# Norm seams grown by VectorE in wider parts, and a GpSimd-only weight split beside the HGRN heads

## What is computed

```
x = x + rms_norm(mixer(rms_norm(x)))      # layer 0: HGRN2 heads | RWKV-7 heads; layer 1: retention | RG-LRU
x = x + rms_norm(swiglu(rms_norm(x)))     # every layer
rms_norm(x, w) = x * rsqrt(mean(x*x) + 1e-6) * w
```

## Time and profile before

| | |
|---|---|
| median of 3 runs | 3651.04 us (3640.59 to 3651.29) |
| the profiled execution | 3655.99 us, span 3654.0 us |
| TensorE busy | 3398.2 us, 93% of the span |
| VectorE, ScalarE, GpSimd busy | 1931.3, 1203.9, 1520.7 us |
| mean granted TensorE clock | 0.948 |

### The profile page before, as it was taken

How to read it: one execution, slowest core, us unless ns; L and a number is a source line. 1 busy time by engine, 2 the same in 40 slices (tenths; PEclk the granted TensorE clock), 3 DMA queues, 4 the chain that set the end, 5 groups by cost and what they waited for, 6 DMA issues and landing times.

```text
span 3654.0 us, 63634 instructions
## 1 busy us (share of the span) xinstructions
PE 3398.2 (93%) x24702; PEld 3263.8 (89%) x24702; DVE 1931.3 (53%) x2531; ACT 1203.9 (33%) x1492; POOL 1520.7 (42%) x888
## 2 busy tenths in 40 slices
PE   7899996858889999999999899999979999999997
PEld 7899985847879999999999799986979999999997
DVE  3544556484776442244456886724784442244456
ACT  3443443232333332233322335321233332233322
POOL 3434552000454444444443445711444445444443
PEclk9999997979899999999999999975999999999999
DMA  4333341000434444444444353532434444444443
GB/s 165 121 131 122 127 135 66 3 25 15 145 109 143 149 149 152 140 149 148 149 156 142 105 208 121 175 130 121 144 100 153 149 155 146 138 150 149 156 151 108
DMA packets 118673, 475.01 MB, mean 130 GB/s; under 512 B 13424, under 2 KB 15088, under 8 KB 115568
## 3 DMA queue, kind: packets, MB, share of 16 engines
q1 hardware_dynamic: 108864, 421.58, 34.4%
q10 hardware_dynamic: 9648, 51.17, 3.6%
HBM read 450.66 MB, written 22.03 MB: 129 GB/s over the span
## 4 chain that ended last, share of the span: by engine, by line
PE 86%; DVE 9%; ACT 3%; issue 2%; POOL 0%; ACTq 0%; DVEq 0%; POOLq 0%
PE ps L330 47%; PE ps L334 24%; DVE w_lo L306 1%; PE ps L1957 1%; PE ps L1977 1%; DVE x_lo L599 1%; PE ps L357 1%; ACT w_hi L295 1%; PE ps L362 1%; PE ps L1066 1%; PE ps L1546 1%; PE ps L1088 1%; PE ps L1495 1%; PE ps L1510 0%; PE ps L1548 0%
## 5 line engine op out<-in xcount | busy, mean ns | idle before, releaser
L306 POOL TENSOR_TENSOR w_lo<-raw,w_hi 128x512 fp32r<-128x512 f32 (+2 forms) x756 | 1389.9, 1840 | 1863.0 <-ACT w_hi L295 1857.0
L330 PE MATMUL ps<-x_hi,w_hi 128*128 128x320 f32 x4832 | 1444.6, 313 | 14.3 <-ACT w_hi L295 7.1
L330 PE MATMUL ps<-x_lo,w_hi 128*128 128x320 f32 x4832 | 1435.0, 311 | 0.0
L295 ACT ACTIVATE w_hi<-raw 128x1024 fp32r<-128x1024 f32 (+1 forms) x756 | 840.4, 1112 | 1643.0 <-PE ps L334 1545.6
L306 DVE TENSOR_TENSOR w_lo<-raw,w_hi 128x512 fp32r<-128x512 f32 (+2 forms) x692 | 630.8, 914 | 701.1 <-ACT w_hi L295 690.5
L330 PEld LDWEIGHTS ps<-x_hi,w_hi 128*128 128x128 f32 x4832 | 914.6, 189 | 23.4 <-ACT w_hi L295 12.7
L330 PEld LDWEIGHTS ps<-x_lo,w_hi 128*128 128x128 f32 x4832 | 914.3, 189 | 0.8
L334 PE MATMUL ps<-x_hi,w_lo 128*128 128x320 f32 x4832 | 811.0, 310 | 25.0 <-DVE w_lo L306 23.3
L334 PEld LDWEIGHTS ps<-x_hi,w_lo 128*128 128x128 f32 x4832 | 734.8, 188 | 31.1 <-POOL w_lo L306 19.3
L330 PE MATMUL ps<-u_hi,w_hi 128*128 128x320 f32 x1408 | 417.7, 311 | 8.3 <-DVE u_lo L711 8.3
L330 PE MATMUL ps<-u_lo,w_hi 128*128 128x320 f32 x1408 | 417.3, 310 | 0.0
(11 more groups left out here) (393 smaller groups left out, 2882.8 us busy)
## 6 DMA issues: line engine op xcount, KB each, us to landing
raw<-in_w_ffn_in SPq DMA_DIRECT2D x352, 512.0 KB, 3.4
raw<-in_w_ffn_out SPq DMA_DIRECT2D x128, 704.0 KB, 4.0
raw<-in_w_in_even SPq DMA_DIRECT2D x116, 512.0 KB, 3.5
raw<-in_w_in_odd SPq DMA_DIRECT2D x96, 512.0 KB, 3.4
raw<-in_w_out_even SPq DMA_DIRECT2D x32, 512.0 KB, 3.4
raw<-in_w_out_odd SPq DMA_DIRECT2D x32, 512.0 KB, 3.4
hS<-in_state_hgrn ACTq DMA_DIRECT2D x4, 1024.0 KB, 5.6
out_hgrn_s<-hS ACTq DMA_DIRECT2D x4, 1024.0 KB, 4.7
```

Of the source, the lines that this page charges most:

```text
L295: nc.scalar.activation(w_hi[s % 2][:, 0:g.kt, :], raw[s % 4][:, 0:g.kt, :], ACT.Copy)\
L306: eng.tensor_tensor(w_lo[s % 2][:, k0:k1, :], raw[s % 4][:, k0:k1, :], w_hi[s % 2][:, k0:k1, :].bitcast(f32), sub).then_inc(sem(f"split_lo ...
L330: nc.tensor.matmul(out, w_hi[s % 2][:, k, :], x[:, kk, :], start=half == 0 and k == 0 and x is xh, stop=False)
```

## The change

In words:

- **Seams.** VectorE does both steps of `grow` itself, in five parts of 1, 1, 2, 2 and 2 of the old ones (`SEAM_PARTS`); GpSimd no longer takes part. ScalarE weights part 0 straight into `x_hi`; for the others it writes the weighted values to `yw` (which lies in the place of `x_lo`) one tile at a time and then rounds the whole part to `x_hi` in one copy. VectorE's `low` is then a plain subtraction over the whole part. ScalarE splits units 2 and 3 together behind part 3, and squares in four instructions of four tiles behind all parts. VectorE alone sums the squares. GpSimd splits its share of units 2 onward in the ordinary loop.
- **Paired heads.** In each half the first part is taken for one unit after the other, so that TensorE begins with the first unit's `w_hi` alone.
- **HGRN.** `lo_dve` of `in_b` becomes 0: GpSimd makes all 8 tiles of each `w_lo` (128x1024). `fill_dve` goes away, VectorE raises the counter for all 100 units at the end (`pass_over`). The head of a group waits on TensorE for ScalarE's read of the state (`pse`) in place of `hgrn_end`.

The core of the diff (the code that it removes is above):

```diff
+        yw = at("yw", XHL0 + KT * T * 4, [P, KT, T])
...
-        dense("in_b", d["w_in_even"], EVEN_TILES - FIRST_TILES, KU_MODEL, 2, FIRST_TILES)
+        dense("in_b", d["w_in_even"], EVEN_TILES - FIRST_TILES, KU_MODEL, 0, FIRST_TILES)
...
         def multiply_head(pe, g, xh, xl, fill):
+            outs = [PS[(g.tile0 + t) % 4][:, 0:T] for t in range(2)]
+
+            def products(s, t, half, k, x):
+                kk = half * g.kt + k
+                if x is xh:
+                    pe.wait_ge(sem("x_hi"), 8 * fill + kk // 2 + 1)
+                else:
+                    x_lo_wait(pe, fill, kk // 2)
+                for a in range(2):
+                    nc.tensor.matmul(outs[t], w_hi[s % 2][:, k + a, :], x[:, kk + a, :],
+                                     start=kk + a == 0 and x is xh, stop=False)
+
+            if g.tile0:
+                pe.wait_ge(sem("tile_out"), g.tile0)
             for half in range(2):
                 units = (g.unit0 + 2 * half, g.unit0 + 2 * half + 1)
...
+                for t, s in enumerate(units):
+                    pe.wait_ge(sem("split_hi"), s + 1)
                     for x in (xh, xl):
+                        products(s, t, half, 0, x)
+                for k in range(2, g.kt, 2):
+                    for x in (xh, xl):
                         for t, s in enumerate(units):
+                            products(s, t, half, k, x)
...
+        SEAM_PARTS = ((0, 1), (1, 2), (2, 4), (4, 6), (6, 8))
+        NPARTS = len(SEAM_PARTS)
+
+        def span(ap, a, b):
+            return ap[:, 2 * a:2 * b, :]
+
         def seam_act(act, n, w, g):
...
+            for q, (c0, c1) in enumerate(SEAM_PARTS):
+                act.wait_ge(sem("seam_y"), NPARTS * b + q + 1)
+                for k in range(2 * c0, 2 * c1):
+                    dst = x_hi[:, k, :] if q == 0 else yw[:, k, :]
+                    ins = act.activation(dst, X[:, k, :], ACT.Copy, scale=vec(w[0], KT * w[1] + k))
+                if q == 0:
+                    ins.then_inc(sem("x_hi"), 1)
+                    continue
+                ins.then_inc(sem("seam_yw"), 1)
+                act.wait_ge(sem("seam_yw"), (NPARTS - 1) * b + q)
+                act.activation(span(x_hi, c0, c1), span(yw, c0, c1), ACT.Copy)\
+                   .then_inc(sem("x_hi"), c1 - c0)
+                if q == 3:
+                    split_hi(act, 0, g.unit0 + 2)
+                    split_hi(act, 0, g.unit0 + 3)
+            for c in range(0, 8, 2):
+                act.activation(span(M, c, c + 2), span(X, c, c + 2), ACT.Square).then_inc(sem("norm_sq"), 1)
...
-        def seam_pool(pool, n, g):
...
         def seam_dve(dve, n, w, g):
...
+            def grow(q):
+                c0, c1 = SEAM_PARTS[q]
+                x = span(X, c0, c1)
+                L(dve.tensor_tensor(x, x, bc(stat[:, 1, :].unsqueeze(1), P, 2 * (c1 - c0), T), mult))
+                dve.tensor_tensor(x, x, span(M, c0, c1), add).then_inc(sem("seam_y"), 1)
+
+            def low(q):
+                c0, c1 = SEAM_PARTS[q]
+                dve.wait_ge(sem("x_hi"), 8 * fill + c1)
+                if q == 0:
+                    for k in range(2):
+                        ins = dve.scalar_tensor_tensor(x_lo[:, k, :], X[:, k, :], vec(w[0], KT * w[1] + k),
+                                                       x_hi[:, k, :].bitcast(f32), mult, sub)
+                else:
+                    ins = dve.tensor_tensor(span(x_lo, c0, c1), span(yw, c0, c1),
+                                            span(x_hi, c0, c1).bitcast(f32), sub)
+                ins.then_inc(sem("x_lo_dve"), c1 - c0)
+
+            grow(0)
+            grow(1)
+            for q in range(NPARTS):
+                if q == 0:
+                    dve.wait_ge(sem("seam_y"), NPARTS * b + 1)
+                low(q)
+                if q + 2 < NPARTS:
+                    grow(q + 2)
+                if q == 3:
                     split_lo(dve, "dve", 0, g.unit0 + 2)
             split_lo(dve, "dve", 0, g.unit0 + 3)
             dve.tensor_scalar(sqt[:, :], PS[7][:, 0:T], RMS_EPS, RMS_EPS * RMS_EPS * D_MODEL, mult, add)
...
+            dve.wait_ge(sem("norm_sq"), 8 + 4 * b + 2)
+            L(dve.tensor_tensor(M[:, 0:4, :], M[:, 0:4, :], M[:, 4:8, :], add))
             split_lo(dve, "dve", 0, g.unit0 + 4)
...
+            for c, k in ((3, 4), (4, 4)):
+                dve.wait_ge(sem("norm_sq"), 8 + 4 * b + c)
+                L(dve.tensor_tensor(M[:, 0:4, :], M[:, 0:4, :], M[:, 4 * c - 4:4 * c, :], add))
+            L(dve.tensor_tensor(M[:, 0:2, :], M[:, 0:2, :], M[:, 2:4, :], add))
             dve.tensor_tensor(M[:, 0, :], M[:, 0, :], M[:, 1, :], add).then_inc(sem("seam_dve"), 1)
             for s in (5, 6, 7):
                 split_lo(dve, "dve", 0, g.unit0 + s)
...
-        def fill_dve(dve):
...
                 pe.wait_ge(sem("tile_out"), 8 * (g + 1))
                 if g:
-                    pe.wait_ge(sem("hgrn_end"), g)
+                    hgrn_wait(pe, "pse", g - 1)
...
-            by_stage(fill_dve(dve), itertools.chain.from_iterable(hgrn_dve(dve, g) for g in range(HGROUPS)))
+            for g in range(HGROUPS):
+                by_stage(hgrn_dve(dve, g))
+            dve.wait_ge(sem("hgrn_end"), HGROUPS)
+            pass_over(dve, plan["in_b"])
```

More of the change, by code:

```diff
@@ L11 @@
-import itertools
 import math
@@ L544, in seam_act @@
             root_act(act, n)
[L546 to L560, removed]
@@ L563, in seam_scale_act @@
+            for c in range(0, 8, 2):
+                act.activation(span(M, c, c + 2), span(X, c, c + 2), ACT.Square).then_inc(sem("norm_sq"), 1)
         def seam_scale_act(act, n):
-            act.wait_ge(sem("seam_dve"), 3 * SEAM[n] + 3)
+            act.wait_ge(sem("seam_dve"), 2 * SEAM[n] + 2)
             act.activation(srow, srow, ACT.Sqrt, scale=1.0 / D_MODEL).then_inc(sem("norm_rms"), 1)
-        def seam_pool(pool, n, g):
[L569 to L578, removed]
-                        pool.wait_ge(sem("seam_acc_pool"), 3 * b + c - 4)
-                split_lo(pool, "pool", 0, g.unit0 + s)
@@ L587, in seam_dve @@
             dve.wait_ge(sem("norm_rms"), MS[n])
-            rms = bc(stat[:, 1, :].unsqueeze(1), P, 2, T)
-            def grow(c):
-                dve.tensor_tensor(part(X, c), part(X, c), rms, mult).then_inc(sem("seam_x"), 1)
-                if c == 0:
-                    dve.wait_ge(sem("seam_x"), 8 * b + 1)
-                    dve.tensor_tensor(part(X, 0), part(X, 0), part(M, 0), add).then_inc(sem("seam_dve"), 1)
-            def low(c):
-                dve.wait_ge(sem("x_hi"), 8 * fill + c + 1)
-                for k in (2 * c, 2 * c + 1):
-                    ins = dve.scalar_tensor_tensor(x_lo[:, k, :], X[:, k, :], vec(w[0], KT * w[1] + k),
-                                                   x_hi[:, k, :].bitcast(f32), mult, sub)
-                ins.then_inc(sem("x_lo_dve"), 1)
-            for c in range(3):
-                grow(c)
-            for c in range(8):
-                if c == 0:
-                    dve.wait_ge(sem("seam_dve"), 3 * b + 1)
-                low(c)
-                if c + 3 < 8:
-                    grow(c + 3)
-                if c == 6:
+            def grow(q):
[23 more added lines that the diff above has]
+                if q == 3:
                     split_lo(dve, "dve", 0, g.unit0 + 2)
@@ L651, in last_norm_dve @@
                 if c % 2:
-                    dve.wait_ge(sem("seam_x"), 24 + c + 1)
+                    dve.wait_ge(sem("seam_x"), c + 1)
                     dve.tensor_tensor(part(X, c), part(X, c), part(M, c), add).then_inc(sem("x_new"), 1)
@@ L818, in fill_act @@
                     act.activation(sh_out[:, n, :], ps[:, 255:T:8], ACT.Copy).then_inc(sem("tile_out"), 1)
-        def fill_dve(dve):
-            g = plan["in_b"]
-            for u in range(g.units):
-                yield fill_stage(u)
-                split_lo(dve, "dve", 0, g.unit0 + u)
         def fill_pe(pe):
@@ L1998, in channel_pool @@
         def channel_pool(pool, l, after):
-            seam_pool(pool, 4 * l + 1, plan[f"up{l}0"])
             for h in range(2):
-                pool_split(pool, plan[f"up{l}{h}"], skip=0 if h else 6)
+                pool_split(pool, plan[f"up{l}{h}"], skip=0 if h else HEAD)
                 pool_split(pool, plan[f"down{l}{h}"])
@@ L2073, in _ @@
             channel_pool(pool, 0, plan["in_c"])
-            seam_pool(pool, 3, plan["in_c"])
-            pool_split(pool, plan["in_c"], skip=6)
+            pool_split(pool, plan["in_c"], skip=HEAD)
             pool_split(pool, plan["in_d"])
```

26 lines of the change are left out of this document (3 added, 23 removed).

## The result

The changed kernel takes 3618.56 us in the median of four runs (3618.26 to 3619.56), the kernel before 3651.16 beside it (3640.59 to 3655.90). The ratio is 0.9916 with a 95% interval of 0.9897 to 0.9935: 0.8% faster. The forecast was 3624 with a range of 3604 to 3642.

What follows compares the result with a forecast made beforehand. TensorE, busy 93% of the span, was taken as the bound, with time to win only where it stands. HGRN 16.3 plus three seams 11.1 made 27.4 us less: 3628.6, or 3624 carried to the median; range 3604 to 3642.

Steps and rivals of the forecast that it cites:

- TensorE's waits beside HGRN: Beside HGRN, 18.3 us of waits for VectorE's `w_lo` go; GpSimd being late costs 2 us.
- the slower rival: Beside HGRN, VectorE holds GpSimd's longer instructions, which take over some 4 us: 17 us slower, 3668; chance 0.06.
- The head wait: At the head of an HGRN group, the new wait costs nothing and brings nothing.
- `w_hi` waits "stay": Beside HGRN, the 3.4 us that TensorE waits for `w_hi` remain.
- The sum 18.3 - 2 = 16.3: HGRN stage: `w_lo` waits gone less new GpSimd delay, 16.3 us less; bounds 20 and 5 less.
- The seam's head: In each seam, the head ends 28.7 us after VectorE's first multiplication in place of 34.75, 6.0 us earlier.
- I take 2.3 us of new wait: Behind each seam's head, TensorE waits 2.3 us for unit 5's part, which stands behind VectorE's four adds of squares.
- 3.7 us less for each seam: Each seam: head 6.0 us earlier less 2.3 of new wait; 11.1 us in all for three.
- one case in which the last 28 products run low: Seam's bad bound: a 3.6 us wait and the last 28 products at low clock, 2.5 us; 0.1 lost.
- the first rival: Seams win nothing, partly as TensorE's clock there is low whenever it has stood; HGRN gives 16.3 less, 3635; chance 0.17.
- The 1.49 us of a 128x1280 step: In the seam, VectorE's 128x1280 step was put at 1.49 us, from 0.81 for 640 and 1.22 for 1024.
- the seams give nothing: Only HGRN wins, 16.3 us less, 3635, with more VectorE work and later squares in the seams; chance 0.17.
- both give their best: HGRN 20 and seams 18 us less, with no new wait behind the adds and shrunken `w_hi` waits: 3613; chance 0.20.

Runs made afterwards that it cites:

- the rest alone: The changed kernel with its HGRN edits taken back, leaving the seams and paired heads: 3647.75 us, ratio 0.9986 to the kernel before.
- narrow parts: The changed kernel with eight seam parts of two tiles each in place of the five of SEAM_PARTS: 3611.89 us, ratio 0.9892 to the kernel before.
- both orders: The changed kernel with each seam's last part ahead of unit 2 and 3 splits, and VectorE's unit 5 and 6 splits between its later adds: 3585.49 us.

## Why the prediction was right in sum, and wrong in its terms

- **TensorE's waits beside HGRN: right.** 18.3 us for VectorE's `w_lo` gone; new waits for GpSimd 3.6 - 1.7 = 1.9 us (forecast 2). The unit at each group's head is late by 0.36 to 0.41 us (forecast 0.4). GpSimd's 128x1024 takes 2.51 us in the mean from 117 to 579 us (at most 2.8 forecast), so the slower rival's condition did not come near. The head wait was worth nothing, as said.
- **`w_hi` waits "stay": failed by what was read.** From 117 us on they did (3.4, then 3.1). The longest, 3.67 us at 106.93, lay ahead of the stretch that I read. It came from VectorE's part of the first 12 units: without it 1.4 us are left there. Bringing these units back costs 2.9 us.
- **The sum 18.3 - 2 = 16.3: the step that failed.** It took waits for the whole cost, and put TensorE's busy time at nothing without a reason. Idle time fell by 18.8 us, busy time by 9.4. The 88 later units alone cost 19.7 us when brought back, 15.9 of it idle time and 3.8 busy time; the first twelve cost 2.9. That is 22.6 of the 28.2. The stage of the kernel with the rest alone is 4.0 us shorter with no HGRN edit, and 1.6 are left, less than the 2.3 by which the stage's end differs among the kernels in which GpSimd makes all of `w_lo` and VectorE does no idle work. What the busy time goes with is shown in part: of the 20 waits for `w_lo` in the kernel before only two, of 2.08 us at 116.68 and of 2.46 us at 508.87, have a clock under 1.00 in the eight microseconds behind them. So it is no price of every wait, and most of it stays open.
- **The seam's head: nearly right.** It ends 29.2 us after the first multiplication (28.7) and is 5.5 us shorter (6.0). Wide steps take 1.48 us (1.49). The new order of the products is worth nothing, as forecast for the three other heads.
- **"I take 2.3 us of new wait": right in place, 2.74 in size.** VectorE held by GpSimd was to be seen in the earlier trace rows (its instruction ended 0.28 us behind GpSimd's, not with it); its adds take 2.5 us beside GpSimd's splits. The Trainium skill (SBUF — State Buffer, Who interferes with whom) has the two engines share a port pair that one locks at a time; these adds agree, 2.5 us against 1.48 alone.
- **"3.7 us less for each seam": the other step that failed.** The idle time fell by 3.6. The busy time rose by 2.5, and 1.1 was left: 49 products ran at the lower clock where 38 had. The clock had been put into a bound, as one case in which the last 28 products run low, and not into the sum. Two places show it: the products behind the 2.74 us wait (2.47 us for eight, 1.34 usual), where moving one split wins 1.3 us of busy time, and half 0, in which narrow parts win 3.6 us without any idle time less. Nor is the clock in a seam "low whenever it has stood", as the first rival has it: behind the 2.56 us wait at 1070.82 of the earlier trace rows it is at full speed.
- **The 1.49 us of a 128x1280 step: a term that was right and asked the wrong question.** It counted what VectorE saves by wide parts. With narrow parts VectorE works 3 us more, TensorE gets an unbroken row of parts, and each seam is 3.6 us shorter.
- **The sum: luck.** HGRN gave 11.9 us more than forecast, the seams 8.2 less, and 5.1 came from stretches that the forecast put at nothing. The rival *the seams give nothing* (16.3 less, 3635) was nearly right on the seams; on HGRN *both give their best* came nearest with 20, and was still 8 short.

## What to carry to other kernels

Don't take a wait of TensorE for the whole of what its cause costs: cut the two profiles at products that both have, and compare length, idle and busy time stretch by stretch; a total that agrees proves no term. Where TensorE is fed part by part, try parts with which it finds the next one ready, even if the feeding engine does more work in sum. And when a version comes out faster than its edit explains, look in the stretches without an edit before crediting it: here 17.6 of 33 us lay there.

## What the runs showed of the hardware that was not expected

The same wait can cost a low clock or nothing. In the kernel before, TensorE waits 2.47 us at 248.24 and 2.46 us at 508.87, both for `w_lo`; ten microseconds about each:

```profile
246.00:256.00 10.00, 7.76 (x53) 7.42 (x54) 7.28 (x12) 5.09 (x6) 5.45 (x3) 1.00 0.46 167
508.00:518.00 10.00, 9.13 (x42) 8.48 (x43) 7.04 (x12) 2.69 (x5) 4.28 (x5) 0.66 0.50 167
```

Behind the first the clock stays at full speed, behind the second it falls to a mean of 0.66. In the kernel with the HGRN edits taken back the same two waits (2.46 us each) stand 2.4 and 0.9 us earlier, and it is the other way round:

```profile
245.00:255.00 10.00, 9.18 (x52) 8.84 (x53) 5.76 (x11) 5.09 (x6) 3.89 (x3) 0.83 0.46 159
507.00:517.00 10.00, 9.06 (x62) 8.72 (x63) 8.22 (x14) 4.33 (x7) 5.43 (x6) 1.00 0.54 174
```

So stretches at half speed move about in code that no edit touched: 3.9 us of busy time in this stage at equal idle time, 18.8 from the second seam to the third. Whether the shift by a microsecond or two does it, or each execution has its own, these traces cannot tell, one of each kernel. The kernel before took 3633.09 us in one execution, at a mean clock of 0.954, and 3656.30 in another beside it, at 0.947. The Trainium skill (TensorE: Matmul & The Clock Gate, Part 1: The HAM clock gate) says that the same kernel can have a different number of slow products from run to run; these two executions agree. Its figure of under 1% of a typical kernel span is for the slow start; here the clock also falls later on, behind waits, and its mean over the kernel before is 0.948. What decides it here was not tried, and whether a delay put in on purpose would win the 17.6 us again stays open. So does the kernel with narrow parts and both orders, which was not run.
